# Norm sums on 128 columns in four column groups, with the factor spread from one row, in a two-block transformer kernel

## The reference

```python
def rms_norm(x, gain):
    xf = x.astype(jnp.float32)
    y = xf * lax.rsqrt(jnp.mean(xf * xf, axis=-1, keepdims=True) + NORM_EPS)
    return (y * gain.astype(jnp.float32)).astype(x.dtype)

# hybrid_layer, twice
h = rms_norm(x, g_pre)                            # pre-norm
... rms_norm(o, sub_gain) * (1.0 - lambda_init)   # diff_attention: one norm for each of 4 heads of width 128
return x + rms_norm(y, g_post)                    # post-norm

# second_block, for layer 0 (Hyena, MoE) and layer 1 (window attention, MoE)
h_l = rms_norm_2(lat, norm1_w[layer]) * (1.0 + mod_l[1]) + mod_l[0]   # the same for the context
h_l = rms_norm_2(lat, norm2_w[layer]) * (1.0 + mod_l[4]) + mod_l[3]   # the context in layer 0 alone
return rms_norm_2(lat, final_norm_w)
```

## Time and profile before

| | |
|---|---|
| median of 3 runs | 3804.66 us (3802.55 to 3804.95) |
| the profiled execution, its own time | 3799.08 us |
| its span, first to last instruction | 3797.3 us |
| mean granted TensorE clock | 0.955 of full |
| busy: PE, DVE, ACT | 91%, 33%, 17% of the span |
| moved by DMA | 588 MB, 155 GB/s on average, up to 420 GB/s in the second MoE |

### The profile page before, as it was taken

The page is one execution under the profiler, slowest core; times in us unless marked ns, Lnnn a source line. Parts: engine busy times, 40 slices in busy tenths (PEclk is TensorE's granted clock), DMA queues, the critical chain, the costliest instruction groups (busy, mean ns, idle before and its releaser), DMA issues. The chain is left out here.

```text
span 3797.3 us, 33327 instructions
## 1 busy us (share of the span) xinstructions
PE 3450.7 (91%) x13514; PEld 1577.6 (42%) x13514; DVE 1242.7 (33%) x2281; ACT 657.0 (17%) x1420; POOL 0.2 (0%) x4
## 2 busy tenths in 40 slices
PE   7999788999989799898977699999998998699998
PEld 3444343344344344454745433333333553333332
DVE  1110672111084334753564312121224572211112
ACT  1000441000053211110111211111002261111111
POOL 0000000000000000000000000000000000000000
PEclk9999999999999899999978899999999999799999
DMA  3333101233300212101311177767782102299995
GB/s 145 133 133 150 72 1 70 96 133 133 152 26 23 79 69 94 47 23 51 143 46 46 76 299 282 274 266 267 291 307 97 45 1 98 116 420 420 420 419 233
DMA packets 86528, 588.05 MB, mean 155 GB/s; under 512 B 12440, under 2 KB 13371, under 8 KB 15972
## 3 DMA queue, kind: packets, MB, share of 16 engines
q1 hardware_dynamic: 78624, 572.56, 38.2%
q10 hardware_dynamic: 7748, 13.30, 1.0%
HBM read 583.73 MB, written 2.10 MB: 154 GB/s over the span
## 5 line engine op out<-in xcount | busy, mean ns | idle before, releaser
L453 PE MATMUL ps<-mem 128*128 128x512 f32 x1152 | 506.8, 599 | 17.1 <-DVE mem L570 17.1
L1672 PE MATMUL ps<-mem 128*64 128x512 f32 x2048 | 467.4, 599 | 1.3 <-ACT mem L1619 0.7
L453 PEld LDWEIGHTS ps<-mem 128*128 128x128 f32 x1152 | 219.2, 192 | 301.4 <-issue 298.3
L1024 PE MATMUL ps<-mem 128*128 128x512 f32 (+1 forms) x768 | 253.0, 492 | 7.7 <-ACT mem L879 7.7
L1672 PEld LDWEIGHTS ps<-mem 128*64 128x64 f32 x2048 | 137.1, 137 | 291.1 <-issue 287.6
L1641 DVE SCALAR_TENSOR_TENSOR mem<-ps,mem 128x512 f32<-128x512 f32 x128 | 96.1, 751 | 359.4 <-PE ps L1601 356.7
L1024 PEld LDWEIGHTS ps<-mem 128*128 128x128 f32 x768 | 147.2, 192 | 113.7 <-issue 102.1
L797 PE MATMUL ps<-mem 128*128 128x512 f32 x384 | 167.1, 592 | 0.0
L450 PE MATMUL ps<-mem 128*128 128x512 f32 x384 | 167.0, 594 | 0.0
L1291 PE MATMUL ps<-mem 128*128 128x512 f32 (+1 forms) x384 | 142.2, 532 | 7.3 <-POOLq L174 7.3
L514 ACT ACTIVATE mem<-ps 128x512 f32<-128x512 f32 x48 | 28.7, 598 | 688.0 <-PE ps L453 688.0
(11 more groups left out here) (294 smaller groups left out, 3941.9 us busy)
## 6 DMA issues: line engine op xcount, KB each, us to landing
mem<-in_moe_w SPq DMA_DIRECT2D x384, 1024.0 KB, 7.9
mem<-in_w_in SPq DMA_DIRECT2D x48, 1024.0 KB, 9.1
mem<-in_ada_w SPq DMA_DIRECT2D x48, 1024.0 KB, 6.7
mem<-in_hy_w_in SPq DMA_DIRECT2D x24, 1024.0 KB, 6.4
mem<-in_w_out SPq DMA_DIRECT2D x12, 1024.0 KB, 8.9
mem<-in_k_win_l SPq DMA_DIRECT2D x8, 1024.0 KB, 6.9
mem<-in_hy_w_out SPq DMA_DIRECT2D x8, 1024.0 KB, 6.6
mem<-in_sw_w_in SPq DMA_DIRECT2D x6, 1024.0 KB, 5.8
```

The source lines that it names most:

```text
L453: m = mm(ps[:, j % 4, :], Wc[s][:, k, t * P:(t + 1) * P], HTL[:, k, :], start=(k == 0), stop=(k == KD - 1))
L1024: m = mm(ps[:, j % 4, 0:L], Wc[s][:, k, (j % 4) * P:(j % 4 + 1) * P], H[:, k, :], start=(k == 0), stop=(k == KD - 1))
L1672: m = mm(ps[64 * x:64 * x + 64, pair, :], lat(k), w[x][:, k % 4, :], start=(k == 0), stop=(k == KD - 1))
```

## The change

The sums of a norm are now made in groups of 128 tokens: for 512 tokens four matmuls, each with 32 columns of ones and 128 moving columns, whose outputs lie on rows 0, 32, 64 and 96 and the 31 below each, in the same 128 columns of one bank (`pe_sums`); for 256 tokens two matmuls with 64 columns. Root and reciprocal then work on 128 x 128. `pe_spread` brings the factor back to all partitions: for each group one matmul with one row of ones and one row of the factor, into one bank for each group; DVE reads the factor there, in PSUM, while it scales. A small root of one column (`act_load_root`) is put ahead of ACT's wait for the sums. For the heads, one bank takes the sums of all four; ACT takes one root of 128 x 512; block 4 of the output projection comes ahead of the head sums, the spreads come after blocks 6 and 7, and block 0 waits for `h_ready` 4; DVE inverts all four heads and waits for the fourth spread before it scales the first. In `sw_a` the context's spread comes after the third tile.

The diff, cut. What is left out names the new semaphores and the banks (`norm_banks` 2 to 5 and 2 to 3 in `hy_a`, `GATE_BANKS` 0 to 3 and 6 to 7 in `moe_a`, `SW_BANKS` 2 to 5 and 6 to 7, banks 0 to 3 in the final norm) and passes them to `pe_norm` and `dve_mod_norm`; `dve_final` scales in the same way as the others.

```diff
@@ -377,26 +377,60 @@
 
 
 
+        def act_root(A, roots, sums, n):
+            act(roots, sums, ACT.Sqrt, bias=eps_col, scale=1.0 / n).then_inc(A.mark("rstd"), 1)
+
+        def act_load_root(A):
+            act(MISC[:, 4:5], MISC[:, 1:2], ACT.Sqrt).then_inc(A.mark(), 1)
+
         def act_norm(A, src, sq, rs, n, bank, turn):
             for k in range(0, KD, 2):
                 act(sq[:, k, :], src[:, k, :], ACT.Square).then_inc(A.mark("squares"), 1)
+            act_load_root(A)
             A.e.wait_ge(S["stat"], turn)
-            act(rs, ps[:, bank, 0:n], ACT.Sqrt, bias=eps_col, scale=1.0 / D).then_inc(A.mark("rstd"), 1)
+            act_root(A, rs[:, 0:P], ps[:, bank, 0:P], D)
 
         def dve_squares(A, src, sq):
             for k in range(1, KD, 2):
                 tt(sq[:, k, :], src[:, k, :], src[:, k, :], ALU.mult).then_inc(A.mark("squares_v"), 1)
 
-        def pe_norm(A, sq, n, bank, turn):
+        def pe_sums(bank, x, start, stop, at=0):
+
+            groups = x.shape[-1] // P
+            rows = P // groups
+            for g in range(groups):
+                m = mm(ps[rows * g:rows * g + rows, bank, at:at + P], ONES[:, 0:rows], x[:, g * P:(g + 1) * P],
+                       start=start, stop=stop)
+            return m
+
+        def pe_spread(A, rs, n, banks, at=0):
+
+            rows = P // (n // P)
+            for g, bank in enumerate(banks):
+                m = mm(ps[:, bank, at:at + P], ONES[rows * g:rows * g + 1, :], rs[rows * g:rows * g + 1, 0:P],
+                       start=True, stop=True)
+            m.then_inc(A.mark("spread"), 1)
+
+        def spread(banks, at=0):
+
+            return ps[:, banks[0]:banks[-1] + 1, at:at + P]
+
+        def blocks(x):
+
+            return x.rearrange("p (g t) -> p g t", t=P)
+
+        def pe_norm(A, sq, rs, n, bank, turn, banks=None):
             for k in range(KD):
                 A.e.wait_ge(S["squares_v" if k % 2 else "squares"], (turn - 1) * 4 + k // 2 + 1)
-                m = mm(ps[:, bank, 0:n], ONES, sq[:, k, :], start=(k == 0), stop=(k == KD - 1))
+                m = pe_sums(bank, sq[:, k, :], k == 0, k == KD - 1)
             m.then_inc(A.mark("stat"), 1)
-
-        def dve_recip(A, rs, turn):
+            if banks:
+                A.e.wait_ge(S["inverted"], turn)
+                pe_spread(A, rs, n, banks)
+
+        def dve_invert(A, rs, turn):
             A.e.wait_ge(S["rstd"], turn)
-            nc.vector.reciprocal(rs, rs).then_inc(A.mark(), 1)
-            A.e.wait_ge(*A.last)
+            nc.vector.reciprocal(rs[:, 0:P], rs[:, 0:P]).then_inc(A.mark("inverted"), 1)
 
 
         hm = Map(AR_)
...
@@ -434,8 +468,11 @@
             kind, w, t = HK[j]
             return {"q": QT, "k": KT, "g": GT, "v": VN}[w][:, kind * 4 + t, :]
 
+        NORM_BANKS = (3, 4, 5, 6)
+
         def pe_hyb_proj(A, st):
-            A.e.wait_ge(S["rstd"], 1)
+            A.e.wait_ge(S["inverted"], 1)
+            pe_spread(A, RS, T, NORM_BANKS)
             for j in range(len(HK)):
                 if j % 4 == 0:
                     s = st.get()
...
@@ -500,7 +537,7 @@
 
         def act_hyb_proj(A, l):
             e = A.e
-            act(RS, ps[:, 7, :], ACT.Sqrt, bias=eps_col, scale=1.0 / D).then_inc(A.mark("rstd"), 1)
+            act_root(A, RS[:, 0:P], ps[:, 7, 0:P], D)
 
             wff = a["w_ff"][bass.ds(l, 1)].rearrange("o p n -> (o p) n")
             e.dma_start(v(WFF_, KD * 8), wff).then_inc(S["const2_in"], 16)
...
@@ -565,9 +602,10 @@
         def dve_hyb_proj(A, l):
             LSV = v(LS_, DEPTH, N_LV)
             nc.vector.tensor_copy(v(LV_, N_LV), LSV[:, bass.ds(l, 1), :].rearrange("p o n -> p (o n)")).then_inc(A.mark(), 1)
-            dve_recip(A, RS, 1)
+            dve_invert(A, RS, 1)
+            A.e.wait_ge(S["spread"], 1)
             for k in range(KD):
-                stt(HTL[:, k, :], XT[:, k, :], lv("g_pre", k), RS, ALU.mult, ALU.mult).then_inc(A.mark("h_ready"), 1)
+                stt(blocks(HTL[:, k, :]), blocks(XT[:, k, :]), lv("g_pre", k), spread(NORM_BANKS), ALU.mult, ALU.mult).then_inc(A.mark("h_ready"), 1)
             A.e.wait_ge(S["const_in"], 48)
             nc.vector.tensor_copy(half_words(MASK_, 4 * P), v(TMP_ + 512, 512)).then_inc(A.mark(), 1)
 
...
@@ -782,22 +820,26 @@
 
 
         def pe_hyb_out(A, st):
-            for h in range(4):
-                A.e.wait_ge(S["squares"], h + 1)
-                mm(ps[:, h, :], ONES, SQS[:, h, :], start=True, stop=True).then_inc(A.mark("stat"), 1)
             for n, c in enumerate(OUT_ORDER):
                 s = st.get()
 
                 for b in ((4, 5, 6, 7, 0, 1, 2, 3) if n == 0 else range(KD)):
-                    if n == 0 and b < 4:
-                        A.e.wait_ge(S["rstd"], b + 1)
+                    if n == 0 and b == 0:
+                        A.e.wait_ge(S["h_ready"], 4)
                     for k in range(4):
-                        if b == 0 and n == 2:
-                            A.e.wait_ge(S["h_ready"], k + 1)
                         m = mm(ps[:, b, :], Wr[s][:, k, b * P:(b + 1) * P], GT[:, 4 * c + k, :],
                                start=(n == 0 and k == 0), stop=(n == 2 and k == 3))
                         if b == 0 and k == 0 and n:
                             m.then_inc(S["w_used"], 2)
+                    if n == 0 and b == 4:
+                        for h in range(4):
+                            A.e.wait_ge(S["squares"], h + 1)
+                            m = pe_sums(0, SQS[:, h, :], True, True, at=h * P)
+                        m.then_inc(A.mark("stat"), 1)
+                    if n == 0 and b in (6, 7):
+                        for h in (0, 1) if b == 6 else (2, 3):
+                            A.e.wait_ge(S["inverted"], h + 1)
+                            pe_spread(A, RSH[:, h, :], T, HEAD_BANKS, at=h * P)
                     if n == 2:
                         m.then_inc(A.mark("psum_full"), 1)
                         if b == KD - 1:
...
@@ -808,14 +850,19 @@
                     st.next()
             pe_post_stat(A, KD - 2)
             pe_post_stat(A, KD - 1)
+            A.e.wait_ge(S["inverted"], 5)
+            pe_spread(A, RS, T, POST_BANKS)
             pe_next_stat(A, 4 + KD)
             end_phase(A)
+
+        HEAD_BANKS = (0, 1, 2, 3)
+        POST_BANKS = (1, 2, 3, 4)
 
         def pe_post_stat(A, k):
             if k == 0:
                 A.e.wait_ge(S["a_ready"], 1)
             A.e.wait_ge(S["squares"], 4 + k + 1)
-            m = mm(ps[:, 0, :], ONES, SQY[:, k, :], start=(k == 0), stop=(k == KD - 1))
+            m = pe_sums(0, SQY[:, k, :], k == 0, k == KD - 1)
             if k == KD - 1:
                 m.then_inc(A.mark("stat"), 1)
 
...
@@ -823,25 +870,26 @@
 
             for k in range(KD):
                 A.e.wait_ge(S["squares"], first + k + 1)
-                m = mm(ps[:, 7, :], ONES, SQ[:, k, :], start=(k == 0), stop=(k == KD - 1))
+                m = pe_sums(7, SQ[:, k, :], k == 0, k == KD - 1)
             m.then_inc(A.mark(), 1)
 
         SQS = v(QT_ + 2048, 4, 512)
-        RSH = v(QT_ + 4096, 4, 512)
+        RSH = v(QT_ + 4096, 4, P)
         YS = v(HT_, KD, 512)
         SQY = v(QT_, KD, 512)
 
         def act_hyb_out(A):
             for h in range(4):
                 act(SQS[:, h, :], QT[:, h, :], ACT.Square).then_inc(A.mark("squares"), 1)
-            for h in range(4):
-                A.e.wait_ge(S["stat"], h + 1)
-                act(RSH[:, h, :], ps[:, h, :], ACT.Sqrt, bias=eps_col, scale=1.0 / P).then_inc(A.mark("rstd"), 1)
+            act_load_root(A)
+            A.e.wait_ge(S["stat"], 1)
+            act_root(A, RSH.rearrange("p h t -> p (h t)"), ps[:, 0, :], P)
             for b in range(KD):
                 A.e.wait_ge(S["psum_full"], b + 1)
                 act(SQY[:, b, :], ps[:, b, :], ACT.Square).then_inc(A.mark("squares"), 1)
-            A.e.wait_ge(S["stat"], 5)
-            act(RS, ps[:, 0, :], ACT.Sqrt, bias=eps_col, scale=1.0 / D).then_inc(A.mark("rstd"), 1)
+            act_load_root(A)
+            A.e.wait_ge(S["stat"], 2)
+            act_root(A, RS[:, 0:P], ps[:, 0, 0:P], D)
             for k in range(KD):
                 A.e.wait_ge(S["b_ready"], k + 1)
                 act(SQ[:, k, :], XT[:, k, :], ACT.Square).then_inc(A.mark("squares"), 1)
...
@@ -849,16 +897,21 @@
 
         def dve_hyb_out(A):
             for h in range(4):
-                dve_recip(A, RSH[:, h, :], h + 1)
-                stt(QT[:, h, :], QT[:, h, :], SMALL[:, 8:9], RSH[:, h, :], ALU.mult, ALU.mult).then_inc(A.mark(), 1)
+                dve_invert(A, RSH[:, h, :], 1)
+            A.e.wait_ge(S["spread"], 4)
+            for h in range(4):
+                q = blocks(QT[:, h, :])
+                stt(q, q, SMALL[:, 8:9], spread(HEAD_BANKS, h * P), ALU.mult, ALU.mult).then_inc(A.mark(), 1)
                 A.e.wait_ge(*A.last)
                 tt(GT[:, h, :], GT[:, h, :], QT[:, h, :], ALU.mult).then_inc(A.mark("h_ready"), 1)
```

(27 more changed lines are left out.)

16 lines of the change are left out of this document (9 added, 7 removed).

## The result

The changed kernel takes **3760.47 us** (median of 4 runs, 3757.69 to 3761.81) against 3804.8 us (3802.55 to 3806.01) of the kernel before on the same chip: ratio 0.9883, 95% interval 0.9866 to 0.9900. The forecast was 3761, with a range of 3746 to 3788. So the two traces differ by 37.3 us in span where the medians differ by 44.3, and a few us of any sum over one pair of traces are scatter.

What follows compares the result with a forecast made beforehand. TensorE, busy 91% of the span, was taken to bound the kernel: matmul streams plus waits on norm chains. Ten places summed to -43.3 us, giving 3761 against the median; its own range 3750 to 3772, stated as 3746 to 3788 in the result.

Steps and rivals of the forecast that it cites:

- Overlap of narrow passes: Norm sums: four column groups overlap, so one code row k costs 0.22 or 0.43 us instead of 0.86 or 1.71.
- Rival A: Norm sums: narrow passes limited by their issue, 0.06 us each, so 3787 us in all; chance 0.15.
- Rival C: Norm sums and spreads: no overlap between narrow passes, so slower, +17.6 us, 3822 us; chance 0.04.
- place 9: Norm of the second MoE layer: gain wholly covered by TensorE's wait for the router's DMA, 0 us.
- Place 4: Head norms, twice: slower, since block 0 waits for VectorE's four products after the last spread; +5.1 each, +10.2 us.
- Places 2 and 3: Pre-norm of the second layer, -1.8 us, and the post-norm, twice, 6.5 us faster each, -13.0 us.
- Place 5: Hyena's latent norm: earlier root and shorter chain, less 0.15 us for a small matmul, -8.1 us.
- Place 7: First MoE layer's norms: latent 6.0 us and context 2.1 us earlier, 2.5 lost at the low clock; -5.6 us.
- Place 6: Hyena's context norm: gain stops where a matmul waits for a constant's DMA, -2.8 us.
- Places 8 and 10: Window attention's norms, -8.1 us, and the final norm, -7.3 us.
- Rival B: Latent Hyena norm and window attention: more is covered than seen, 16 us go, 3778 us; chance 0.07.
- Rival D: Whole kernel: nothing moves by over 0.2%, from Rival A with a longer stand in the head norms; chance 0.04.

Runs made afterwards that it cites:

- e3: Changed kernel, sums of norms with their own squares started only after the last square, all passes of one column group before the next: 3795.32 us.
- e1: Changed kernel with the reciprocal of every norm but the head norms taken three times in a row: 3781.35 us.
- e9: Changed kernel with the head norms put back as in the kernel before, all other norms narrow: 3748.85 us.
- e5: Changed kernel with VectorE scaling all four heads first and multiplying by the gates afterwards, spreads still behind blocks 6 and 7: 3754.58 us.
- e4: Changed kernel with VectorE scaling all four heads before the gates, and spreads moved to follow blocks 5 and 6: 3744.93 us.
- e6: Changed kernel with the second MoE layer's router weights loaded early, in the window attention's first phase: 3742.80 us.
- e7: Kernel before, with the second MoE layer's router weights loaded early, in the window attention's first phase: 3791.25 us.

## Why the prediction was right, and where it was off

- **Overlap of narrow passes** (0.22 us for a row k at the high clock, 0.43 at the low one): right. Two groups of four start 110 ns apart at the high clock and 213 at the low one, so a row k takes 0.22 and 0.43 us. Rival A (0.06 us a pass where I had 0.027) falls with the 35 ns, waits for squares included. Rival C falls with both, and e3 makes what it described, passes in line, at 108 ns each (213 at the low clock). The Trainium skill ("TensorE: Matmul & The Clock Gate", Part 1, "Wait — 56ns, not 53.3ns?") puts some 62 ns of the sequencer's time on each MATMUL with hardware decode off. At that price 64 passes would take 4.0 us, an estimate from that page; they took 2.21, so that bound is not at work here.
- **Reciprocal** 0.95 us, forecast and measured; e1 shows that it was path time everywhere but at place 9. **Root** 0.35 to 0.37 (0.37). **Spread** 0.50 at the high and 0.81 us at the low clock (0.6 and 0.9). **Scaling from PSUM** 0.75 us (0.75).
- **Place 4, +10.2 forecast, 12.3 in the traces and 11.6 by e9.** The mechanism, banks 0 to 3 held until DVE has done all four heads, is shown by e5 and e4, and the stand is 5.76 us for 5.7. The term that was too small is the low clock after it, 2.3 in the forecast and 3.0 in the trace (6.0 us of PE's work in the stretch, at half speed); that is 0.7 of the 1.0 us a layer, and 0.3 more is the last spread, which ends 17.0 us after the first square for 16.7.
- **Places 2 and 3, -14.8 forecast, -13.9 measured.** The sums inside the stream gave 1.5 for 1.7 a layer and the chain behind them 3.9 for 4.0; the rest is in the next norm's sums and the pre-norm.
- **Place 5, -8.1**, came out to the digit, though ACT idled 2.10 us before the root: I had counted the sums at the low clock (3.6 us), and that is what they took.
- **Place 7, -5.6 forecast, -6.6 measured.** The charge of 2.5 us for a router at the low clock was wrong: the router's products took 10.49 us in both kernels. Most of it was offset by the context's sums: they took 3.68 us at the low clock and ended 2.8 us after the last square, where I had 0.45. So the context side, with its spread at 0.49 for 0.9, gained 0.1 us for 2.1. The latent side gained 6.4 for 6.0; that the table load, not the sums, ended the wait before its root cost nothing against the forecast.
- **Place 6, -2.4 for -2.8**, but not for the reason given. I had the load of a constant as the limit. In the trace of after no DMA ends a wait there; the small matmul runs right behind the spread, and the projection waits for the norm's own chain:

```profile
1782.51 0.49 PE L410 MATMUL ps<-mem 1*128 1x128 f32 x4 [1.46 <-DVE mem L433]
1782.93 0.64 PE L1070 MATMUL ps<-mem 33*64 33x256 f32 x2
...
1784.21 3.32 PE L1080 MATMUL ps<-mem 128*128 128x256 f32 x7 [0.64 <-ACT mem L932]
```

  The sums of the context, at the low clock for most of their 3.37 us, are what this chain waited for. That the number came out near is luck.
- **Places 8 and 10** within 0.3.
- **Place 9, 0**: right, and for the reason given. The wait for the router's weights grew, and e6 and e7 show some 5 to 7 us of gain lying under it.
- **Rival B** (more covered than seen) falls: no place with a gain to give gave less than 0.8 of its forecast. **Rival D** needed A, and falls with it.

The mechanism was right but for places 6 and 7. That the median came within 1 us is in part luck: the traces give -40.9 for the places where I had -43.3, and the streams between move by up to 2 us each.

## What to carry to other kernels

A statistic that is the same in every row can be made on a fraction of the columns if each column group of the array takes its own block of tokens, but write the passes so that neighbours are of different groups: the order of the loops alone was worth 19 us here, where the whole change brought 44. Before a norm is made faster, ask what the next stream waits for last (here a DMA covered one norm of ten). Where the short form puts its result into PSUM banks that an accumulation wants next, free the banks before doing anything else with the data: the stand cost 5.8 us a layer and the clock after it 3.0 more. Halving the stand saved only the standing (e5); the 3 us of the clock were saved only when no stand was left (e4).

## What the runs showed of the hardware that I had not expected

- Float32 passes of 128 columns in one column group start 213 ns apart at the low clock and 108 to 113 at the high one (e3), a quarter of what 512 columns take. Four groups of 32 array columns in turn put four passes into one such step: 53 ns each at the low clock, 27 at the high one. Two groups of 64 put two into it. For the 32 passes of the window attention's context sums, in the stream at the high clock, that is 1.97 us against 3.33 one group after the other.
- Halving the stand (5.76 to 2.85 us) left PE's work at the low clock nearly as it was (6.03 to 5.77 us). Without a stand there was none.
- The same small load of a constant took 5.0 to 5.2 us from issue to use in eleven kernels and 7.6 in one that differs from the changed kernel in twelve missing one-element instructions.
